# Neighbourhood attention: turning the weights by a product with a diagonal of inverse sums

## The reference, cut to what matters

```python
s_loc = jnp.einsum('bhrnqd,bhrnkd->bhrnqk', qg, kg).astype(jnp.float32) * scale + bias[None]
s_ctx = jnp.einsum('bhrnqd,bhkd->bhrnqk', qg, k_ctx).astype(jnp.float32) * scale
p = jax.nn.softmax(jnp.concatenate([s_loc, s_ctx], axis=-1), axis=-1).astype(v.dtype)
o = (jnp.einsum('bhrnqk,bhrnkd->bhrnqd', p[..., :nloc], vg)
     + jnp.einsum('bhrnqk,bhkd->bhrnqd', p[..., nloc:], v_ctx))
```

## Time and profile before

| | |
|---|---|
| median of three runs | 1739.69 us (1739.23 to 1740.97) |
| the profiled execution | 1740.12 us, its span 1738.3 us |
| TensorE matmul busy | 1674.2 us, 96% |
| VectorE busy | 1102.8 us, 63% |
| ScalarE busy | 735.0 us, 42% |
| GpSimd busy | 213.5 us, 12% |
| mean granted TensorE clock | 0.982 of full |

### The profile page before, as it was taken

How to read it: one execution, slowest core, us unless ns; L and a number is a source line. 1 busy time by engine, 2 the same in 40 slices (tenths; PEclk the granted TensorE clock), 3 DMA queues, 4 the chain that set the end, 5 groups by cost and what they waited for, 6 DMA issues and landing times.

```text
span 1738.3 us, 26413 instructions
## 1 busy us (share of the span) xinstructions
PE 1674.2 (96%) x10650; PEld 1494.3 (86%) x10650; DVE 1102.8 (63%) x1726; ACT 735.0 (42%) x1238; POOL 213.5 (12%) x204
## 2 busy tenths in 40 slices
PE   5999999899999999999999999999999999999997
PEld 3999864689999999999989974445999999999996
DVE  3777666856757777785587647886585653332345
ACT  3433235755653312213345745654475332221333
POOL 0000014432100000000120402443310000000011
PEclk7999999999999999999999989999999999999998
DMA  9455212131556456473412500002154722222231
GB/s 334 155 174 166 82 47 61 29 104 31 149 176 176 121 170 194 122 205 99 116 38 49 149 13 1 1 1 83 52 146 134 206 74 73 73 74 80 79 85 61
DMA packets 266794, 181.63 MB, mean 104 GB/s; under 512 B 26237, under 2 KB 239090, under 8 KB 265650
## 3 DMA queue, kind: packets, MB, share of 16 engines
q1 hardware_dynamic: 266674, 179.96, 35.7%
HBM read 173.75 MB, written 3.62 MB: 102 GB/s over the span
## 4 chain that ended last, share of the span: by engine, by line
PE 81%; DVE 9%; ACT 3%; issue 3%; DMA 2%; SPq 1%; POOL 0%; DVEq 0%; ACTq 0%; POOLq 0%
PE ps L824 21%; PE ps L826 21%; PE ps L825 21%; PE ps L1397 3%; PE ps L1407 2%; DMA ada_a<-in_w_ada 1%; PE ps L990 1%; PE ps L992 1%; PE ps L991 1%; DVE w_lo L575 1%; PE ps L1024 1%; PE ps L1006 1%; PE ps L878 1%; ACT km L1923 1%; ACT w_hi L566 1%
## 5 line engine op out<-in xcount | busy, mean ns | idle before, releaser
L566 ACT ACTIVATE w_hi<-stage 128x1024 fp32r<-128x1024 f32 (+1 forms) x176 | 184.7, 1052 | 615.8 <-PE ps L826 500.1
L575 DVE TENSOR_TENSOR w_lo<-stage,w_hi 128x1024 fp32r<-128x1024 f32 (+1 forms) x176 | 216.8, 1233 | 281.9 <-ACT w_hi L566 281.7
L824 PE MATMUL ps<-hM_hi,w_lo 128*128 128x320 f32 x952 | 295.2, 310 | 0.0
L826 PE MATMUL ps<-hM_hi,w_hi 128*128 128x320 f32 x952 | 294.2, 309 | 0.0
L825 PE MATMUL ps<-hM_lo,w_hi 128*128 128x320 f32 x952 | 294.1, 309 | 0.0
L824 PE MATMUL ps<-h_hi,w_lo 128*128 128x320 f32 x824 | 255.9, 311 | 2.6 <-DVE h_lo L2497 2.6
L826 PE MATMUL ps<-h_hi,w_hi 128*128 128x320 f32 x824 | 254.6, 309 | 0.0
L825 PE MATMUL ps<-h_lo,w_hi 128*128 128x320 f32 x824 | 254.6, 309 | 0.0
L2742 POOL TENSOR_TENSOR rstd<-rstd,sq 128x320 f32<-128x320 f32 x73 | 77.3, 1064 | 960.8 <-ACT sq L1490 959.2
L824 PEld LDWEIGHTS ps<-hM_hi,w_lo 128*128 128x128 f32 x952 | 178.7, 188 | 3.4 <-issue 3.4
L825 PEld LDWEIGHTS ps<-hM_lo,w_hi 128*128 128x128 f32 x952 | 178.7, 188 | 0.1
(11 more groups left out here) (412 smaller groups left out, 3525.8 us busy)
## 6 DMA issues: line engine op xcount, KB each, us to landing
stage<-in_w_mlp_out SPq DMA_DIRECT2D x83, 512.0 KB, 4.2
stage<-in_w_mlp_in SPq DMA_DIRECT2D x80, 512.0 KB, 4.6
slab_mlp<-in_w_ada SPq DMA_DIRECT2D x28, 1024.0 KB, 5.3
stage<-in_w_in_ac SPq DMA_DIRECT2D x28, 512.0 KB, 3.9
slab_ac<-in_w_ada SPq DMA_DIRECT2D x12, 1024.0 KB, 6.1
ada_a<-in_w_ada SPq DMA_DIRECT2D x8, 1024.0 KB, 16.6
stage<-in_w_out_ac SPq DMA_DIRECT2D x8, 512.0 KB, 4.1
stage<-in_w_out_c SPq DMA_DIRECT2D x8, 512.0 KB, 4.3
```

What stands on the lines that cost most here:

```text
L566: nc.scalar.activation(hi_place(n)[:, 0:width], stage[:, n % STAGE, 0:width], ACT.Copy)\
L575: nc.vector.tensor_tensor(lo_place(n)[:, 0:width], stage[:, n % STAGE, 0:width], hi_place(n)[:, 0:width].bitcast(F32), ALU.subtract).then_ ...
L824: mm(out, lo[:, k], xh, start=j == 0, stop=False)
L826: last = mm(out, hi[:, k], xh, start=False, stop=j == k_tiles - 1)
```

## The change

The scaling of the weights by VectorE is removed. In its place VectorE multiplies the identity by the inverse sums, which gives a diagonal of 128 by 128 per head; there is a new tile of four such diagonals, two tiles of the attention in turn. The turn is now a matmul of the unscaled weights with this diagonal as moving operand: column q of the result is the row of query q times its inverse sum. VectorE waits, from tile 2 on, until the turn of two tiles ago has read the diagonal that it is about to write.

```diff
+        [inverse_at] = lay(136, ("inverse_at", [P, 4, P], F32))
...
                     for kt in range(3 if t % 5 < NB else 1):
-                        last = nc.tensor.transpose(ps[:, 4 + e, P * kt:P * (kt + 1)],
-                                                   pA[:, 2 * (t % 3) + e, P * kt:P * (kt + 1)], ident[:])
+                        x = 2 * (t % 3) + e
+                        last = mm(ps[:, 4 + e, P * kt:P * (kt + 1)], pA[:, x, P * kt:P * (kt + 1)], inverse_at[:, 2 * (t % 2) + e, :],
+                                  start=True, stop=True)
                     last.then_inc(na_t, 1)
...
             def na_norm(t, e):
-                w, x = 384 if t % 5 < NB else TC, 2 * (t % 3) + e
+                x = 2 * (t % 3) + e
                 dve.wait_ge(na_e, 2 * t + e + 1)
+                if t >= 2:
+                    dve.wait_ge(na_t, 2 * (t - 2) + e + 1)
                 link(nc.vector.reciprocal(smA[:, 2, x:x + 1], smA[:, 1, x:x + 1]))
-                ts(pA[:, x, 0:w], pA[:, x, 0:w], smA[:, 2, x:x + 1], None, ALU.mult).then_inc(na_p, 1)
+                ts(inverse_at[:, 2 * (t % 2) + e, :], ident[:], smA[:, 2, x:x + 1], None, ALU.mult).then_inc(na_p, 1)
```

## The result

The changed kernel takes 1743.23 us (median of 10 runs, 1741.51 to 1744.97), the kernel before 1739.37 us in the 10 runs beside it (1737.53 to 1741.04). The ratio is 1.0022 with a 95% interval of 1.0013 to 1.0032: slower by 3.9 us. The forecast was 1742.5 us, +2.8. The profiled execution took 1742.82 us, its span is 1740.7 us.

The account below looks back on a forecast made before the run. TensorE was taken to bound tiles 5 to 12, VectorE the stage from tile 12; 2.0 us late at tile 19 plus 0.7 at the end, rounded to 2.8, on 1739.7 gave 1742.5 us, range 1739.6 to 1745.8.

Parts of the forecast that it names:

- (a): Tiles 0 to 4, at low clock: the costlier turns make tile 5 start 1.6 us late.
- (b): Tiles 5 to 12, TensorE bound: 3.1 us added, 1.6 taken up by holes; tile 12 starts 3.1 us late.
- if time changes behind the stage: Sign that the prediction is wrong: time changing after the neighbourhood attention stage, behind which TensorE runs without a gap.
- VectorE beginning to wait for TensorE from tile 13 on: Sign that the prediction is wrong, in the stretch where VectorE was taken to set the pace.
- Step 1: TensorE's turn as a product: two records for one, 1.35 us per tile of six, +0.55; 9.4 us in all.
- Step 2: VectorE's scaling narrowed from 384 to 128 columns: 0.14 us less each, 0.28 per tile, 4.5 us in all.
- (c): Tile 12 to the end, VectorE bound: -1.7 us from scalings, +1.1 from waits at tiles 15 and 18.
- Step 3: VectorE's added wait for the turn two tiles ago: costed at nothing, at most 1 us.
- (d): End of the stage: turns of tiles 18 and 19 lie on the path, +0.55 and +0.16 us.
- Rival A: Start of the stage: products bring full clock back earlier, tile 5 on time; 1740.8 us, +1.1, chance 27%.
- Rival B: From tile 12 on, the two-tile chain with the longer turn sets the pace; 1745.4 us, +5.7, chance 22%.
- Rival C: The product costs as a turn, its two records overlapping, and VectorE's gain counts; 1737.9 us, chance 6%.

Follow-up runs that it names:

- e1: Kernel before with the turn as a product with the identity, VectorE still scaling the weights; 1743.66 us, ratio 1.0029 to the kernel before.
- e9: Changed kernel with VectorE's splitting of the second piece of projection weights moved behind its last reciprocals; 1740.07 us, ratio 1.0007 to the kernel before.
- e7: Second trace of e1, no further edit; its stage takes 72.85 us.
- e5: e1 with VectorE's scaling removed as well, reciprocals kept, division left out of the result; 1740.16 us, ratio 1.0003 to the kernel before.
- e2: Changed kernel with the turn kept a transposition, diagonals made but unused, division left out; 1737.58 us, ratio 0.9988 to the kernel before.
- e4: Kernel before with unscaled weights transposed, inverse sums spread by narrow products, VectorE multiplying the output tile at its store, two smaller moves; 1736.94 us, ratio 0.9989.
- e10: e4 with GpSimd's low part of the fourth head pair moved behind its last bias tiles; 1735.34 us, ratio 0.9975 to the kernel before.
- e3: Changed kernel with weights and diagonals in the shorter f32 format (fp32r); 1742.3 us, ratio 1.0021 to the kernel before.

## Why the prediction was right, and which term was off

- *What bounds the kernel and the stage.* Right in that TensorE set the pace in the first half and VectorE in the second. The time lies in the range, 0.7 us above the forecast and 1.1 above it in the difference (+3.9 for +2.8). It is at 1.0022 just on the slower side of 0.2%, to which a third of the chance was given; the interval, 1.0013 to 1.0032, has both sides in it.
- *The size, and luck.* The stage alone lost 4.9 us, so the sum was 2.1 short: 0.4 in (a), 1.1 in (b) and 0.6 from tile 12 on. That the total came out nearer is owed to what lies outside. The prediction named "if time changes behind the stage" as a sign of being wrong, and the time did change there, by 1.7 us between the first traces and 0.8 between the second. It also named VectorE beginning to wait for TensorE from tile 13 on; this it does at the two tiles where its own sum had it, and for 0.17 us at tile 19; its waits for the last values grew from 1.6 to 3.2 us.
- *Step 1, the product.* Right in kind: two records for one, cadence 0.11 us. This is the term that was mis-sized. A tile of six takes

```profile
322.70 1.60 PE L1116 MATMUL ps<-inverse_at,pA 128*128 128x128 f32 x12
324.24 0.44 PE L1135 MATMUL ps<-pTA,nv 128*64 128x128 f32 x4
```

  324.24 - 322.70 = 1.54 us, where 1.35 was taken and 1.42 was the upper bound. The twelve records are 12 x 0.112 = 1.34 us; the gap between the records of the two heads and the one behind the last are another 0.20. The turn of 0.80 us already had 0.15 of such gaps over its six records, and the sum left hardly any of it for the product. The row of layer 1 that gave the price has hardly any: one run of eight records, and the next matmul 0.03 us behind the start of the last. A context tile costs 0.64 (+0.27), where +0.16 was taken. At the low clock

```profile
305.04 2.91 PE L1116 MATMUL ps<-inverse_at,pA 128*128 128x128 f32 x12
307.88 1.23 PE L1099 MATMUL ps<-kn,oT 64*128 64x256 f32 x4
```

  it is 2.84 us in place of 2.64. With +0.74 and +0.27 the prediction's own step (b) gives 5 x 0.74 + 2 x 0.27 - 1.6 = +2.6; measured +2.58. So against the first trace of the kernel before the 1.6 us of holes that were to be taken up were right, and the whole error of (b) is this term (against the second trace, with 21.97, it is +2.10).
- *Step 2, the scaling.* The width costs what was said: 0.21 us free of GpSimd (from 348.24 to the next start at 348.45), 1.45 us behind it at 350.47 above, more than the 0.7 to 0.9 that was named. The mean is 554 ns, against 666 and 690 before. But where it was to count, 1.7 us in (c), the product left little for it: 0.24 us in tiles 12 to 19 between the second trace of e1 and the changed kernel.
- *Step 3, the added wait.* Right: no row shows it.
- *(a).* Tiles 0 to 5 became 1.98 us longer, for +1.6: the product at the low clock costs more than was taken. The low clock lasts 10.2 us in both traces but lies 1.1 us earlier in the stage of the changed kernel (it sets in ahead of the first product), so that its third turn runs at full clock throughout. (In the kernel before the clock came back at 312.4 and not 312.6: a mean of 0.79 over that microsecond is 0.42 us at 0.50.)
- *(c) and (d).* VectorE's own starts went nearly as forecast from tile 12 to 19. Counted from the first scores, its minimum of tile 12 is 3.90 us late (2.6 forecast) and that of tile 19 is 3.40 (2.0): -0.5 between them, for -0.6. The waits that were forecast, 0.2 us at tile 15 and 0.9 at tile 18, are there:

```profile
349.31 0.56 DVE L2376 CUSTOM_DVE_ANT_0 nt<-ps,bm 128x384 f32<-128x384 f32 x1 [0.19 <-PE ps L1106]
...
359.51 0.56 DVE L2376 CUSTOM_DVE_ANT_0 sq<-ps,bm 128x384 f32<-128x384 f32 x1 [0.95 <-PE ps L1106]
```

  What was wrong is the path. TensorE added 8 x 0.74 + 2 x 0.27 = 6.5 us from tile 12 on, not 4.7, its idle time there fell from 7.1 to 2.3 us, and its own starts set the end: 4.56 us late at tile 12, 4.58 at tile 19, 4.88 at the projection. VectorE's gain was covered but for 0.24 us.
- *Rival A, the clock comes back earlier.* The low clock of the changed kernel is as long as in the first trace of the kernel before, so A's time did not come. The other traces don't settle what A rests on: at the stage's start the low clock lasted 10.2, 10.2, 10.2, 10.2, 6.8 and 3.4 us with two-record products (the changed kernel twice, e9, e7, e5, e1) and 10.2, 6.8, 10.2, 10.2 and 13.7 us with transpositions (the kernel before twice, e2, e4, e10). The Trainium skill, TensorE: Matmul & The Clock Gate, Part 4: PE-mode transpose, says that transposes don't count as busy time for the clock gate, which had spoken for this rival; these runs neither bear it out nor exclude it.
- *Rival B.* Its size, +5.7, is near the stage's +4.9, but it placed the loss from tile 12 on, and there the stage became only 0.3 us longer. The loss came in front of it, 4.6 us by tile 12, through TensorE's own work (24.07 us with VectorE at 21, 19.4 or 11.9 us).
- *Rival C.* Falls with the 208 records and their cadence.

## What to carry to other kernels

In these traces a transposition through TensorE has one record a block in f32 and a product with a diagonal two, 0.80 and 1.54 us for six blocks. Folding a scaling into the turn can pay only where TensorE has room for the second records; here, with both engines near full, VectorE's saving was covered. To price a short group of matmuls, count the records and add the gaps that such a group has at its semaphores, read from a row with the same neighbours: the 0.20 us of such gaps, almost left out here, are the error of step 1. A factor that is constant along the summed axis can be applied behind the sum, on the narrow output: here 128 columns at the store in place of 384 columns ahead of the turn, with the turn left alone.

## What the runs showed of the hardware

The time of this kernel moves by one to three us from one execution to the next, and much of it goes with how long TensorE's clock is low. In 1000 to 1060 us, in layer 1, whose code is the same in all of these kernels, the kernel before, the changed one and e9 had

```profile
1000.00:1060.00 60.00, 52.41 (x275) 39.70 (x275) 34.41 (x51) 27.07 (x48) 9.24 (x10) 0.83 0.03 10
```

```profile
1000.00:1060.00 60.00, 52.41 (x292) 39.99 (x291) 35.06 (x51) 29.93 (x51) 12.12 (x14) 0.89 0.03 10
```

```profile
1000.00:1060.00 60.00, 50.73 (x295) 37.11 (x293) 35.24 (x51) 29.69 (x53) 10.62 (x12) 0.94 0.03 9
```

mean clocks of 0.83, 0.89 and 0.94, and 1373.9, 1372.2 and 1369.5 us from the projection's first matmul to the end of the span. This one stretch is a poor measure: seven traces have 0.89 in it, with rests of 1371.1 to 1374.0 us. The low clock of the whole rest, added up over stretches of 2 us, tells more:

| trace | low clock behind the stage | the rest |
|---|---|---|
| e9 | 19.6 us | 1369.5 us |
| e1, e2 | 25.8, 25.8 | 1371.1, 1371.4 |
| e5, the changed kernel twice, e7 | 27.2, 27.4, 27.3, 27.9 | 1372.8, 1372.2, 1372.3, 1372.2 |
| the kernel before, second trace, and e4 | 29.1, 29.6 | 1373.0, 1374.0 |
| e3, the kernel before | 31.7, 33.2 | 1373.1, 1373.9 |
| e10 | 34.8 | 1376.1 |

So the changed kernel's trace, which gets back 1.7 of its 4.9 us there, has 5.8 us less of low clock behind the stage than the kernel before. Over 10 runs of each the difference is +3.9. Both of its traces have less low clock there than both of the kernel before; whether the change brings that about, or chance, stays open.

The shorter f32 format, one record a product, came with a mean clock of 0.72 and 0.70 in the last two stretches of the stage, and with a mean of 0.975 to 0.982 over the whole of each of its twelve executions. The changed kernel, with two records a product, had 1.00 in these stretches.
